# Hybrid decoder layer on one core: order of operand and weight loads, distance of the gate rows, pace of the weight pieces in the last pass, and who forms their lower parts

## What is computed

```
h = RMSNorm(x) ;  p = h @ w_in + b_in
p = [q_a k_a v_a z_a | q_m k_m v_m o_m z_m | i_m f_m | g_a g_b]
attn   = sliding-window attention with sinks over q_a, k_a, v_a
hm     = chunkwise mLSTM (4 heads of 256) over q_m, k_m, v_m, i_m, f_m
y_a = attn * silu(z_a) ;  y_m = sigmoid(o_m) * hm * silu(z_m)
merged = sigmoid(g_a) * (y_a @ w_pa) + sigmoid(g_b) * (y_m @ w_pb)
x_new  = x + RMSNorm(merged @ w_out)
```

## Times and profile of the kernel before

| | |
|---|---|
| median of 3 runs | 2826.03 us (2825.18 to 2828.23) |
| the profiled execution | 2831.79 us, span 2830.0 us |
| mean granted clock of PE | 0.988 |
| busy, share of span: PE | 2735.1 us, 97% |
| DVE | 1642.1 us, 58% |
| ACT | 939.0 us, 33% |
| POOL | 702.4 us, 25% |
| DMA queue of SP and the other hardware queue | 56.2% and 16.4% of 16 engines |

### The profile page before, as it was taken

One profiled execution on the slowest core, in us unless ns is written; L12 is line 12 of the kernel. 1 busy time (PEld: TensorE's weight loads), 2 busy tenths in 40 slices (PEclk: granted clock), 3 DMA queues, 4 the chain that ended last, 5 costly groups with the idle time before them and its releaser, 6 DMA issues. The chain is left out here.

```text
span 2830.0 us, 46426 instructions
## 1 busy us (share of the span) xinstructions
PE 2735.1 (97%) x15620; PEld 2287.2 (81%) x15620; DVE 1642.1 (58%) x4145; ACT 939.0 (33%) x2291; POOL 702.4 (25%) x1022
## 2 busy tenths in 40 slices
PE   6999999999999999999999999999999999999898
PEld 5888888888887867787887887888887888788786
DVE  5776665555663245465556546556337662577887
ACT  5774443444441021132122113114123231333533
POOL 3333533533551022202212222221100000022222
PEclk9999999999999999999999999999999999999999
DMA  8664566555767898888889888898896577957634
GB/s 316 236 219 159 173 200 208 170 181 168 228 221 259 280 339 279 289 271 291 292 270 301 283 283 292 265 291 279 290 328 218 197 266 248 325 191 242 212 149 149
DMA packets 410526, 697.47 MB, mean 246 GB/s; under 512 B 31778, under 2 KB 177575, under 8 KB 410260
## 3 DMA queue, kind: packets, MB, share of 16 engines
q1 hardware_dynamic: 298724, 526.72, 56.2%
q10 hardware_dynamic: 108848, 158.46, 16.4%
q0 software_dynamic: 2720, 9.32, 1.0%
HBM read 526.87 MB, written 169.48 MB: 246 GB/s over the span
## 5 line engine op out<-in xcount | busy, mean ns | idle before, releaser
L2847 PE MATMUL bank_second<-w_all,a_all 128*128 128x512 f32 x736 | 299.7, 407 | 12.2 <-DMA a_all<-hh_t 8.3
L2850 PE MATMUL bank_second<-w_all,a_all 128*128 128x512 f32 x736 | 289.5, 393 | 0.0
L2849 PE MATMUL bank_second<-w_all,a_all 128*128 128x512 f32 x736 | 288.9, 392 | 0.0
L2430 ACT ACTIVATE mx_qkt<-st_bank_t 128x512 f32<-128x512 f32 x68 | 40.8, 600 | 570.8 <-PE st_bank_t L2870 562.7
L2847 PE MATMUL bank_first<-w_all,a_all 128*128 128x512 f32 x496 | 200.2, 404 | 11.7 <-DMA a_all<-hh_t 3.9
L2850 PE MATMUL bank_first<-w_all,a_all 128*128 128x512 f32 x496 | 195.1, 393 | 0.0
L2849 PE MATMUL bank_first<-w_all,a_all 128*128 128x512 f32 x496 | 194.5, 392 | 0.0
L2847 PE MATMUL bank_third<-w_all,a_all 128*128 128x512 f32 x464 | 188.5, 406 | 4.3 <-DMA a_all<-sh_t 3.0
L308 PE MATMUL bank_first<-w_all,a_all 128*128 128x384 f32 x536 | 186.5, 348 | 0.0
L2850 PE MATMUL bank_third<-w_all,a_all 128*128 128x512 f32 x464 | 181.2, 390 | 0.0
L2849 PE MATMUL bank_third<-w_all,a_all 128*128 128x512 f32 x464 | 180.8, 390 | 0.0
(11 more groups left out here) (404 smaller groups left out, 7251.0 us busy)
## 6 DMA issues: line engine op xcount, KB each, us to landing
a_all<-sh_t SPq DMA_DIRECT2D x224, 512.0 KB, 5.4
a_all<-hh_t SPq DMA_DIRECT2D x180, 512.0 KB, 5.7
a_all<-hh_t ACTq DMA_DIRECT2D x104, 512.0 KB, 4.9
h_raw<-l_blocks_in ACTq DMA_DIRECT2D x64, 512.0 KB, 5.9
difs_t<-h_raw ACTq DMA_DIRECT2D x64, 512.0 KB, 6.6
st_waiting<-difs_t SPq DMA_DIRECT2D x118, 256.0 KB, 6.5
st_waiting<-l_blocks_in SPq DMA_DIRECT2D x84, 256.0 KB, 6.2
hh_t<-a_all SPq DMA_DIRECT2D x34, 512.0 KB, 6.0
```

What stands on the lines that cost most here:

```text
L2847: T.matmul(bank_view(bank, at), hi, weight_row(k, at, 0, t), start=fresh and t == 0, stop=False, skip_group_check=True)
L2849: T.matmul(bank_view(bank, at), hi, weight_row(k, at, 1, t), start=False, stop=False, skip_group_check=True)
L2850: last = T.matmul(bank_view(bank, at), lo, weight_row(k, at, 0, t), start=False, stop=t == KH - 1, skip_group_check=True)
```

## The change

- In SP's loop `next_operand(q + 3)` now stands ahead of the weight units of step q.
- The gate rows and decay rows of a tile are issued at TURN − 2 instead of TURN − 4.
- `lower_by_dve` is true for every unit from H0 on: seven units in each of H0, H1, H2, H3 and GA, 35 in all, go from POOL (L2260) to DVE (L2525).
- The units of OUT are split at step −6 + 2x/5 instead of −6 + x/3, relative to the start of OUT; lower parts and loads follow.
- In OUT the P2 bank of each of the eight pairs is copied out by ACT, in its own step, instead of DVE.
- In the first stage the mask amask is counted on `order_in` instead of `c_in`: PE waits for three constants instead of four, DVE for three masks instead of two.

```diff
-            sp.dma_start(amask[:, :, :], k.c_amask).then_inc(c_in, 16)
+            sp.dma_start(amask[:, :, :], k.c_amask).then_inc(order_in, 16)
...
-                dve.wait_ge(order_in, 16 * 2)
+                dve.wait_ge(order_in, 16 * 3)
...
-            pe.wait_ge(c_in, 16 * 4)
+            pe.wait_ge(c_in, 16 * 3)
...
-    return kt != 3 if s < PA else True
+    return True
...
-    return N_PROD * s - 6 + (x // 3 if s >= PA else x // 2)
+    return N_PROD * s - 6 + (x * 2 // 5 if s == OUT else x // 3 if s >= PA else x // 2)
...
-                n = TURN.get(q + 4)
+                n = TURN.get(q + 2)
...
             for q in range(-4, Q_ALL + 8):
+                if 6 <= q + LOADED_AHEAD < Q_ALL:
+                    next_operand(q + LOADED_AHEAD)
                 for v in LOADS_AT.get(q, ()):
                     load_unit(v)
-                if 6 <= q + LOADED_AHEAD < Q_ALL:
-                    next_operand(q + LOADED_AHEAD)
...
+                    if i and j == P2 and s == OUT:
+                        act.wait_ge(prod, q)
+                        wait_line(act, N_ITEM * s + i, 0, 0)
+                        A.activation(c[:, 0, 0:LW], bank_x[:, :], ACT.Copy).then_inc(c11_ready, 1)
...
-                    elif s == OUT:
-                        V.tensor_copy(c[:, 0, 0:LW], bank_x[:, :]).then_inc(c11_ready, 1)
-                    else:
+                    elif s != OUT:
```

## The result

The changed kernel takes 2843.4 us (median of 4 runs, 2840.9 to 2847.9), the kernel before 2826.4 us (2825.2 to 2828.2): 1.0067 times the time, 95% interval 1.0054 to 1.0080. The profiled execution took 2840.89 us with a span of 2839.1 us, 9.1 us above the span of before. It was the shortest of its kernel's four, and the profiled one of before, 2831.8 us, was longer than all of that kernel's timed runs, so the two traces show about half of the difference. What follows rests on where in the program the time went.

What follows compares the result with a forecast made beforehand. PE, computing for 97% of the span, was taken to bound the kernel. The terms summed to −3.3 us, so 2826.7 us of span, 2828.5 us profiled and 2822.7 us for the median; range 2816 to 2829.5 with 8 of 10.

Steps and rivals of the forecast that it cites:

- Start, amask: First stage: PE does not wait for this mask and its next step waits for DVE; −0.1 us.
- H0, x = 28: Product 28 of H0: later gate rows let its operand land earlier, so PE's 3.26 us wait goes; −4.2 us.
- x = 36: Product 36 of H0, H1, H2: moved rows delay a late operand, each wait growing 0.7 to 0.85 us; +2.4 us.
- End of GA: Last product of GA: the operand wait shrinks under 1 us, but DVE's later evictions take most back; −2.3 us.
- End of GB: Last product of GB: same edit, with a new PE wait and half clock against it; −0.3 us.
- Start of OUT: First products of OUT: first wait shorter, second longer behind three more upper and lower parts; +1.2 us.
- P2 on ACT: Eight copies go from DVE to ACT, both with slack there; 0 us.
- Lower parts on DVE, and units issued later: Starts of head passes: 35 lower parts fit on DVE, landings move half a us; +0.4, from −1 to +4 us.
- The prediction's own sign of being wrong: Forecast wrong if PE's PA and PB waits stay out, or w_all, w_early waits appear in a head pass's first seven products.
- Rival C: Weights late in the head passes: PE waits at the starts of H1, H2, H3 and GA; +8.3, 2834.3 us; chance 0.1.
- B: DVE doesn't bind after GA and GB, so the whole gain there comes; −14, 2812 us; chance 0.25.
- D: The gain in H0 does not come, as tile 6's rows land late; about 0 to +1, 2826.5 us; chance 0.15.

Runs made afterwards that it cites:

- e6: Kernel before with the gate and decay rows two products later for all tiles as its only edit; 2828.4 us, ratio 1.0006.
- e1: Changed kernel with the weight units of a step ahead of the operand again; 2833.1 us, ratio 1.0014 to the kernel before.
- e4: Kernel before with the operand ahead of the weight units of a step as its only edit; 2837.9 us, ratio 1.0038.
- e8: Kernel before with all lower parts from H0 on by DVE as its only edit; 2824.4 us, ratio 0.9997.
- e9: Kernel before with the operand ahead of the units and the units up to GA loaded one step earlier; 2825.4 us, ratio 0.9997.
- e11: Kernel before, order kept, with SP waiting for prod to reach q before the units, x = 40 of ZM to x = 20 of GA; 2826.7 us.
- e14: Kernel before, units still first, but those of the passes up to GA loaded one step later; 2852.1 us, ratio 1.0094.
- e12: Kernel before with gate rows later for tile 6 of H0 alone and the state loads of x = 32 spread over four steps; 2814.7 us, ratio 0.9960.
- e10: Kernel before with rows later for tile 6 of H0, state loads spread, and operand first at the end of GA; 2814.2 us, ratio 0.9961.
- e5: Kernel before with operands first only from x = 50 in GA and GB, and gate rows later only for tile 6 of H0; 2819.1 us.

## Why the prediction was wrong, point by point

**Start, amask.** Taken at −0.1. PE's wait for the mask is gone, and the next one is for DVE as said. Right, and nothing.

**H0, x = 28.** −4.2 forecast, −4.6 in the changed kernel, −4.3 alone (e6). Right, with its mechanism. On SP, and PE at x = 28, in the changed kernel:

```profile
1118.40 0.80 SPq L2183 DMA_DIRECT2D o_s_wk<-cache_win_k_in  x1
1119.23 0.74 SPq L2183 DMA_DIRECT2D o_s_wv<-cache_win_v_in  x1
1121.40 0.38 SPq L1672 DMA_DIRECT2D a_all<-sh_t  x1
...
1135.46 0.50 PE L2849 MATMUL bank_second<-w_all,a_all 128*128 128x512 f32 x1
```

No wait stands at the product; in the earlier trace rows it was 3.26 us. The times are not earlier than in the earlier trace rows only because PE is 3.1 us later by then.

**x = 36.** +2.4 forecast for three places. The changed kernel has +1.5, +3.5 and −0.4, which is 4.6, e1 +3.8, +3.8 and 0. The term was taken too small: the waits of H0 and H1 grow by 1.5 and 1.9 us where 0.7 to 0.85 had been taken, and a stretch of half clock follows in H1, and in e1 in H0 too. The forecast had named one of +1.5 and left it out of the sum. The wait at H1 in the changed kernel:

```profile
1404.90 0.50 PE L2849 MATMUL bank_first<-w_all,a_all 128*128 128x512 f32 x1 [3.20 <-DMA a_all<-hh_t]
```

and the windows behind it (columns as in the earlier trace rows), the first with a mean granted clock of 0.60:

```profile
1404.90:1409.00 4.10, 4.09 (x11) 0.60 1.07 369
1409.00:1411.30 2.30, 2.30 (x11) 0.97 1.03 328
```

That H2 shows no growth is the fault of the base: in most other kernels this stretch is 2 to 3 us shorter than in the profiled execution of before, also in those that touch nothing there (e4, e8, e9, e11, e14).

**End of GA.** −2.3 forecast, −5.6 seen. The operand now goes ahead of the units, and PE doesn't wait for it:

```profile
2131.43 0.37 SPq L1672 DMA_DIRECT2D a_all<-hh_t  x1
2131.90 2.14 SPq L2088 DMA_DIRECT2D st_waiting<-l_blocks_in  x3
...
2139.39 0.39 PE L2849 MATMUL bank_second<-w_all,a_all 128*128 128x512 f32 x1
...
2163.00 0.47 PE L2849 MATMUL bank_second<-w_early,a_all 128*128 128x512 f32 x1 [1.06 <-DVE st_u L2582]
```

Of the 7.5 us gained up to PA 1, DVE takes 1.9 back, with the new wait for L2582 (L2578 before) that had been forecast. But 5.6 is not what the edit is worth. Kernels without it have this stretch 1.0 (e8), 3.1 (e12), 4.6 (e11), 4.9 (e14), 5.0 (e6) and 5.4 us (e1) shorter too: the profiled execution of before was a slow instance of it. The pair e10 and e12 puts the edit at 0.5 us of 2814, nothing measurable. The forecast's reason (DVE binds behind it) held; its 2.3 is more than that pair shows.

**End of GB.** −0.3 forecast. −4.9 in the changed kernel, −0.4 in e4, +1.1 in e5, with the same order. PE waits in PB for DVE and for POOL's L2292, and it varies between kernels by more than the edit moves. Not settled.

**Start of OUT.** +1.2 forecast, +1.1 seen. ACT and DVE, with the three upper parts behind the root and the three lower parts before the sum, and PE behind them:

```profile
2673.33 1.28 ACT L2383 ACT_TABLE_LOAD   x1
2674.63 0.29 ACT L2383 ACTIVATE st_small<-st_small 128x1 f32<-128x1 f32 x1
2674.83 1.65 ACT L2362 ACTIVATE w_all<-st_waiting 128x512 fp32r<-128x512 f32 x3
...
2679.52 1.89 DVE L2529 TENSOR_TENSOR w_all<-st_waiting,w_all 128x512 fp32r<-128x512 f32 x3
2681.32 0.68 DVE L2582 TENSOR_TENSOR st_u<-bank_second,st_t 128x512 f32<-128x512 f32 x1
...
2682.16 0.77 PE L2849 MATMUL bank_second<-w_early,a_all 128*128 128x512 f32 x1 [6.96 <-DVE st_u L2582]
```

The 1.65 and 1.89 us are the 1.7 and 1.8 of the forecast, and the wait of 6.96 us lies in its "6 to 7 us".

**P2 on ACT.** Taken at 0. Nothing in the traces speaks against it; it was not run alone.

**Lower parts on DVE, and units issued later.** Here the prediction failed. The first half is right: e8 has no loss. The step that failed is the sentence "but the landings, bound by what is in the queue, move by half a us", with its +0.4 and the upper bound of +4 for all starts of head passes. The landings moved by 4 us at x = 26, and the starts cost 18.9. Three things were missed. First, a later issue is a later landing there: in e4 SP issues x = 26 of H1 4.4 us later, measured from the start of product 6, and it lands 4.3 us later. The prediction's rows had landings from the end of GA alone, and none from the start of a head pass. Second, the margin was reckoned from each unit's own product, "over 4 us for all other blocks". From H1 on, what waits in the changed kernel is not that product: it is the eviction or the mixer's step that stands behind the lower part in DVE's stream. For x = 26 and 27 the first margin is over 12 us in the head passes of every kernel, and 5 us or more in GA, and the second is used up. Third, the tightest block was not that of H2: at x = 6 of H0 PE already waited 1.6 us for a lower part in the kernel before, so there was no margin, and in the changed kernel PE waits 3.7 us more for lower parts at the start of H0.

The prediction's own sign of being wrong came: "waits for w_all and w_early appear in the first seven products of a head pass". In H0 of the changed kernel PE waits for w_early at x = 3 and x = 6 and for w_all at x = 5, 5.6 us in all, where it was 1.9 us at x = 6 before. For H1, H2 and H3 the sign stays out, though they lose more than 10 us together: it looked at the products' own weights only.

**The other terms together.** The starts take 18.9 us and the medians differ by 17, so all the rest of the change comes to some −2 us, an estimate from a trace and medians, where the other terms of the sum come to −3.7. That it looks like −10 between the two traces is for the most part the long execution of before.

**The rivals.** Rival C had the right place and sign, "weights late in the head passes", at 2834 with a chance of 0.1. It was priced by the wrong unit (x = 23) and at four starts; 2843 lies beyond it. B, that DVE doesn't bind after GA and GB, did not come, nor did D: the gain at x = 28 of H0 is there.

**The port shared by DVE and POOL.** By the rule on the lock in the Trainium skill ("SBUF — State Buffer", "Who interferes with whom") the term would have been 0 instead of +0.4. e8 gives −0.2 us at the five starts and 0.9997 in time: it cannot tell them apart. What the trace of e8 does show is the small copy itself: its four instances take 0.17 us each, with nothing of POOL running beside them, where they take 0.17 to 1.04 us in the kernel before, and the one of 0.17 is the one with POOL idle. That agrees with the rule, but the time does not show it.

## What to carry to other kernels

A transfer's margin runs to the first instruction that stands behind its consumer in an engine's stream, not to the first use of the data: ACT waits for the landing, DVE for ACT, and PE for an eviction that is queued behind. When two issues in a loop change places, the second inherits the first one's wait and gets its bytes ahead of it. Here the wait alone cost 2.6 us at the five starts and both together 12.8, and moving the second one's step along with it took nearly all of it back. And where a single profile shows a stall of a few us, look at the same stretch in a second kernel that leaves it alone before its removal is counted as a gain.

## What the runs showed of the hardware

The stretch of half clock after a wait is not tied to a length of the wait alone. In the profiled execution of before, a wait of 2.3 us at x = 36 of H2 was followed by one, as this window of it shows:

```profile
1632.96:1636.83 3.87, 3.87 (x10) 0.56 1.06 379
```

The wait of 2.4 us in its OUT was not. In the changed kernel the wait of 1.9 us at x = 36 of H2 was followed by one (a mean granted clock of 0.64 in the 4.1 us behind it), and that of 2.5 us in H0 was not (1.00). In e5 none followed a wait of 3.56 us in OUT, as long as the one that had it before; here the stretch behind that wait (columns as in the earlier trace rows):

```profile
2661.98:2665.40 3.42, 3.37 (x15) 1.00 0.13 47
```

The changed kernel's wait of 6.96 us in OUT was followed by one too; the window from its product to the next has a mean granted clock of 0.60, the 3.4 us behind it 1.00 (columns as in the earlier trace rows):

```profile
2682.16:2686.60 4.44, 4.44 (x12) 0.60 0.00 0
2686.60:2690.00 3.40, 3.40 (x16) 1.00 0.36 77
```

And 12 matmuls after 6.96 us of idle time cost 4.44 us, 1.7 more than a product's 2.72: as much as after the 3.56 us in the kernel before, where the stretch was 3.41 us long. The longer wait did not make it dearer here.
